# Attention in single-pass high and low parts, one head after another, with the division on GpSimd

## The reference, cut to what matters

```python
q = (_rmsnorm(c_q, q_norm) @ w_uq)          # 8 heads of 64 + 32 (rotary)
kv = (_rmsnorm(c_kv, kv_norm) @ w_ukv)      # 8 heads of 64 (key) + 64 (value)
k_rope = _apply_rope(k_r, cos, sin)         # one for all heads
s = (q_nope . k_nope + q_rope . k_rope) * (64 + 32) ** -0.5
p = softmax(s, axis=-1)                     # rows of 512 keys
o = p @ v
```

## Time and profile before

| | us |
|---|---|
| median of 3 runs | 2398.46 (2389.69 to 2399.76) |
| profiled execution | 2398.28 |
| its span | 2396.6 |
| PE busy (matmul) | 1885.3, 79% |
| DVE (VectorE) | 956.1, 40% |
| ACT (ScalarE) | 609.4, 25% |
| POOL (GpSimd) | 592.5, 25% |

### The profile page before, as it was taken

The page is one execution under the profiler, slowest core; times in us unless marked ns, Lnnn a source line. Parts: engine busy times, 40 slices in busy tenths (PEclk is TensorE's granted clock), DMA queues, the critical chain, the costliest instruction groups (busy, mean ns, idle before and its releaser), DMA issues. The chain is left out here.

```text
span 2396.6 us, 21376 instructions
## 1 busy us (share of the span) xinstructions
PE 1885.3 (79%) x7770; PEld 1285.0 (54%) x7770; DVE 956.1 (40%) x1462; ACT 609.4 (25%) x1006; POOL 592.5 (25%) x292
## 2 busy tenths in 40 slices
PE   4989895839991897997765997199689446999997
PEld 3855432724440683542552443178469335888886
DVE  2814455411115552445540111563366361432332
ACT  2233455001110333445301111212420422111111
POOL 3410024221112430012321110244032022444442
PEclk9989996859995998998767999599779867999998
DMA  4110011148843310010117773231000012222221
GB/s 156 68 63 1 19 53 53 44 190 318 312 158 113 145 44 37 1 44 27 53 45 320 293 304 117 88 126 38 8 1 0 5 70 94 92 96 99 94 88 44
DMA packets 42415, 234.85 MB, mean 98 GB/s; under 512 B 9732, under 2 KB 11652, under 8 KB 22612
## 3 DMA queue, kind: packets, MB, share of 16 engines
q1 hardware_dynamic: 32452, 216.47, 23.9%
q0 software_dynamic: 9728, 16.93, 1.9%
q10 hardware_dynamic: 144, 0.26, 0.1%
HBM read 226.00 MB, written 24.41 MB: 104 GB/s over the span
## 5 line engine op out<-in xcount | busy, mean ns | idle before, releaser
L249 PE MATMUL bank<-XS,WS 128*128 128x512 f32 x864 | 201.4, 396 | 20.0 <-POOL WS L395 20.0
L1958 POOL TENSOR_TENSOR WS<-ring,WS 128x2048 fp32r<-128x2048 f32 x32 | 154.6, 4833 | 228.0 <-ACT WS L1950 228.0
L249 PEld LDWEIGHTS bank<-XS,WS 128*128 128x128 f32 x864 | 165.0, 191 | 56.0 <-POOL WS L395 21.4
L1979 PE MATMUL bank<-XS,WS 128*128 128x512 f32 x768 | 177.2, 393 | 14.5 <-POOL WS L1958 14.5
L1997 PE MATMUL bank<-WS,US 128*128 128x512 f32 x768 | 174.7, 389 | 0.0
L1979 PEld LDWEIGHTS bank<-XS,WS 128*128 128x128 f32 x768 | 145.8, 190 | 45.2 <-issue 14.7
L1997 PEld LDWEIGHTS bank<-WS,US 128*128 128x128 f32 x768 | 144.1, 188 | 29.9
L1384 PE MATMUL bank<-XS,WS 128*128 128x512 f32 (+1 forms) x600 | 138.2, 393 | 14.6 <-POOL WS L1438 14.6
L609 POOL TENSOR_TENSOR RM<-ROW,mask 128x512 f32<-128x512 f32 x32 | 41.5, 1301 | 380.4 <-DMA ROW<-gate_rows 318.9
L1384 PEld LDWEIGHTS bank<-XS,WS 128*128 128x128 f32 (+1 forms) x600 | 112.1, 187 | 40.4 <-POOL WS L1438 14.8
L1950 ACT CAST WS<-ring 128x2048 fp32r<-128x2048 f32 x32 | 61.2, 1913 | 283.5 <-PE bank L1979 150.5
(11 more groups left out here) (438 smaller groups left out, 3179.5 us busy)
## 6 DMA issues: line engine op xcount, KB each, us to landing
raw<-in_w_exp SPq DMA_DIRECT2D x16, 2048.0 KB, 10.2
DN<-in_w_exp SPq DMA_DIRECT2D x32, 1024.0 KB, 4.9
GU<-in_w_exp SPq DMA_DIRECT2D x16, 2048.0 KB, 10.3
ring<-in_w_ff SPq DMA_DIRECT2D x32, 1024.0 KB, 4.8
raw<-in_w_in SPq DMA_DIRECT2D x20, 1024.0 KB, 4.8
ring<-in_w_in SPq DMA_DIRECT2D x12, 1024.0 KB, 4.7
raw<-in_w_out SPq DMA_DIRECT2D x8, 1024.0 KB, 4.9
ROW<-gate_rows SPq DMA_DIRECT2D x32, 256.0 KB, 3.2
```

The lines of the kernel that those rows point to most:

```text
L249: last = pe.matmul(m.ps[g % 8][:, :], WS[:, i % 2, hw, at:at + P], XS[:, hx, k, :], start=(step == 0), stop=(step == 3 * KD - 1))
L1958: pool.tensor_tensor(f.WS[:, q % 2, 1, :], f.ring[:, q % 4, :], f.WS[:, q % 2, 0, :].bitcast(F32), ALU.subtract).then_inc(w_low, 1)
L1979: last = pe.matmul(m.ps[mine + u % 4][:, :], f.WS[:, q % 2, hw, k * 256 + c * P:k * 256 + (c + 1) * P], f.XS[:, hx, k, :], start=(n == 0), ...
```

## The change

- Scores (`scores_of`): queries and keys are held as high and low parts in float32r (`QS`, `KS`), three one-pass matmuls of 512 columns replace one float32 matmul. The key's rotary rows are split once.
- Probabilities with values (`values_of`): `VS` and `PT` are split likewise. Two tiles (256 query columns) are taken together: per pair of tiles 4 blocks of 3 terms, 12 matmuls of 256 columns, done in two parts of 6, one part per step. All the tiles of a head go to one bank `O`, which ScalarE copies home once per head.
- The halves are gone. The heads run one by one: the projection of head h+1 is put among the tiles of head h (query at t = 0, key at t = 1), the values' 4 matmuls among the tiles of head 0.
- New splitting work: ScalarE makes high parts (`query_high` at t = 1, `key_high` at t = 2, `PT` high for each tile), VectorE low parts (`key_low` at t = 2, `PT` low for each tile), GpSimd the query's low part.
- The scale goes into the rotary table once (in `constants`); the maximum is negated by the reduction itself, so that L544 goes.
- The product with the reciprocal (L549) moves from VectorE to GpSimd.
- Three score banks instead of four; three `PT` buffers of two tiles; `w_mla` is put in the upper half of `raw` and is loaded after low part 8 instead of 10, and the quarters of `w_out` go to the lower half.

The core of the new stage, in each engine's order:

```diff
@@ tensor, per step (32 tiles + 6)
+                if step < NI:
+                    scores_of(step)
+                    if t == 0 and h + 1 < HEADS:
+                        query(h + 1)
+                    if t == 1 and h + 1 < HEADS:
+                        key(h + 1)
+                    if h == 0:
+                        value(t)
+                if 2 <= step < NI + 2:
+                    turned(step - 2)
+                if step >= 5:
+                    u, part = divmod(step - 5, 2)
+                    if u < 2 * HEADS:
+                        values_of(u, (2 * part, 2 * part + 1))
@@ values_of
+                if ks[0] == 0:
+                    pe.wait_ge(pt_low, 2 * u + 2)
+                    if u == 0:
+                        pe.wait_ge(v_low, NT)
+                    if half == 0 and h >= 1:
+                        pe.wait_ge(head_home, h)
@@ scalar, start and per step
+            inverse(0, m.ps[1], 128)
+            act.wait_ge(kr_done, 1)
+            act.copy(a.KS[64:128, :, 0, :], ...).then_inc(kr_high, 1)
+            inverse(1, m.ps[0], 256)
+            key_high(0)
+            query_high(0)
...
+                if step >= 10 and step % NT == 2 and step // NT <= HEADS + 1:
+                    hp = (step - 10) // NT
+                    act.wait_ge(pv, 4 * (hp + 1))
+                    act.copy(m.XT[64 * (hp % 2):64 * (hp % 2) + 64, hp // 2, :], O[0:64, :]).then_inc(head_home, 1)
+                if step < NI:
+                    act.wait_ge(neg_max, step + 1)
...
+                    act.activation(PR[:, step % 4, :], m.ps[step % 3][:, :], ACT.Exp, ...).then_inc(probs, 1)
+                    if h == 0:
+                        act.wait_ge(v_done, t + 1)
+                        act.copy(a.VS[:, 0, t, :], O[:, :]).then_inc(v_high, 1)
+                    if h + 1 < HEADS:
+                        if t == 1:
+                            query_high(h + 1)
+                        if t == 2:
+                            key_high(h + 1)
+                if 2 <= step < NI + 2:
+                    act.wait_ge(probs_t, i + 1)
...
+                    act.copy(a.PT[:, u % 3, 0, :, ...], m.ps[4 + i % 2][:, :]...).then_inc(pt_high, 1)
@@ vector, per step
+                    dve.reduce_max(a.NM[...], m.ps[step % 3][:, :], AX.X, negate=True).then_inc(neg_max, 1)
+                    if h == 0:
+                        dve.wait_ge(v_high, t + 1)
+                        dve.tensor_tensor(a.VS[:, 1, t, :], O[:, :], a.VS[:, 0, t, :].bitcast(F32), ALU.subtract).then_inc(v_low, 1)
+                    if h + 1 < HEADS:
+                        if t == 0:
+                            query_home(h + 1)
+                        if t == 2:
+                            key_low(h + 1)
+                if 1 <= step <= NI:
...
+                    dve.reciprocal(a.RC[...], a.SM[...]).then_inc(inv_sum, 1)      # tile step - 1
+                if step >= 2:
...
+                    dve.wait_ge(pt_high, i + 1)                                    # tile i = step - 2
+                    dve.tensor_tensor(a.PT[:, u % 3, 1, ...], m.ps[4 + i % 2]..., a.PT[:, u % 3, 0, ...], ALU.subtract).then_inc(pt_low, 1)
@@ gpsimd
+            query_low(0)
+            for i in range(NI):
+                pool.wait_ge(inv_sum, i + 1)
+                pool.tensor_scalar(PR[:, i % 4, :], PR[:, i % 4, :], a.RC[...], None, ALU.mult).then_inc(probs_normed, 1)
+                if t == 1 and h + 1 < HEADS:
+                    query_low(h + 1)
```

More of the change, by code:

```diff
@@ L441, in _ @@
-            for half in range(2):
-                for hh in range(HH):
-                    h = half * HH + hh
-                    if h == 0:
[L446 to L486, removed]
@@ new lines, in query, with key @@
+            def query(h):
+                if h >= 1:
+                    pe.wait_ge(q_home, h)
+                for k in range(2):
+                    last = pe.matmul(Q[:, :], wq[:, k, h * P:(h + 1) * P], mx.CQ[:, k, :], start=(k == 0), stop=(k == 1))
+                last.then_inc(q_done, 1)
+            def key(h):
+                if h >= 1:
+                    pe.wait_ge(k_low, h)
+                pe.matmul(K[0:64, :], wk[:, h * 64:(h + 1) * 64], mx.CQ[:, 2, :], start=True, stop=True).then_inc(k_done, 1)
@@ new lines, in value, with scores_of @@
+            def value(t):
+                if t >= 1:
+                    pe.wait_ge(v_low, t)
+                pe.matmul(O[:, :], mx.CQ[:, 2, t * P:(t + 1) * P], wv, start=True, stop=True).then_inc(v_done, 1)
+            def scores_of(i):
+                h, t = divmod(i, NT)
+                if t == 0:
+                    pe.wait_ge(k_low, h + 1)
+                    pe.wait_ge(q_low, h + 1)
+                if i == 0:
+                    pe.wait_ge(kr_low, 1)
+                if i >= 3:
+                    pe.wait_ge(probs, i - 2)
+                for n, (hk, hq) in enumerate(TERMS):
+                    last = pe.matmul(m.ps[i % 3][:, :], a.QS[:, h % 2, hq, t * P:(t + 1) * P], a.KS[:, h % 2, hk, :], start=(n == 0), stop=(n == 2))
+                last.then_inc(scores, 1)
@@ new lines, in turned, with values_of @@
+            def turned(i):
+                pe.wait_ge(probs_normed, i + 1)
+                if i >= 2:
+                    pe.wait_ge(pt_low, i - 1)
+                for k in range(NT):
+                    last = pe.transpose(m.ps[4 + i % 2][:, k * P:(k + 1) * P], PR[:, i % 4, k * P:(k + 1) * P], m.ident[:, :])
+                last.then_inc(probs_t, 1)
+            def values_of(u, ks):
+                h, half = divmod(u, 2)
+                if ks[0] == 0:
[4 more added lines that the diff above has]
+                        pe.wait_ge(head_home, h)
+                n = 0
+                for k in ks:
+                    for hv, hp in TERMS:
+                        last = pe.matmul(O[0:64, half * 256:(half + 1) * 256], a.VS[:, hv, k, h * 64:(h + 1) * 64], a.PT[:, u % 3, hp, k, :],
+                                         start=(k == 0 and n == 0), stop=(k == NT - 1 and n == 3 * len(ks) - 1))
+                        n += 1
+                last.then_inc(pv, 1)
@@ L498, in _, with inverse @@
[L498 to L508, removed]
[L509 to L518 removed]
+            def inverse(c, bank, width):
+                act.wait_ge(sums, c + 1)
+                link(act.activation(RS[c], bank[:, :], ACT.Ln, scale=1.0 / width, bias=1e-6))
+                act.activation(RS[c], RS[c], ACT.Exp, scale=-0.5).then_inc(inv_rms, 1)
```

183 lines of the change are left out of this document (107 added, 76 removed).

## The result

The changed kernel takes 2424.11 us (median of 4 runs, 2421.87 to 2425.73) against 2398.72 (4 runs, 2389.69 to 2399.76): ratio 1.0112, 95% interval 1.0092 to 1.0132. It is slower, by more than can be taken for no change, and by less than the 2440 forecast. The profiled execution took 2421.87 us, span 2420.1, which is 23.5 more than the span before.

A forecast was written before the change was run, and what follows sets the result against it. TensorE was taken to bound the attention stage at 2.51 us a tile, with in-order waits binding after the change. 2398.3 + 26.7 (stage) + .5 (table scale) + 15 (clock) = 2440 us; own range 2428 to 2455, 8-in-10 range 2392 to 2468.

The forecast's parts named there:

- the rival in which the clock holds: Rival for the attention stage: TensorE's gaps bring no half clock, so the kernel takes 2425 us; chance .23.
- The two waits: TensorE stalls per head: 1.8 us before values at t = 1 (head copy), 2.5 before transposes at t = 3 (GpSimd's product).
- The product at 1.57: GpSimd's one-operation product of probabilities with the reciprocal, 128x512, was taken to last 1.57 us.
- TensorE's work per tile: Attention tile on TensorE: scores .80, transposes .53, values .87, so 2.20 us instead of 2.51; 11.7 per head with projections.
- my 297.8: Forecast length in us of the attention stage over both layers, 148.9 each, 26.7 over the earlier 271.1.
- The clock: Half clock on TensorE after its gaps, 1.7 us of work lost each; two of three gaps counted, 15 us.
- 16 us from one head's first scores to the next: Sign of being right, in the attention stage's timeline: a head takes 16.0 us against 13.8 before.
- Start and end: Attention stage's edges: 18.0 us to first scores; head 7 10.0 to its last maximum plus a drain of 8.9.
- The other stages: Only the attention stage was to change; any other stage moving by more than 2 us was a sign of being wrong.
- The short terms: Rival: GpSimd's product .77, no change-over between TensorE's groups, 14.4 us per head; 2405, no change; chance .17.
- The half clock feeds itself: Rival: gaps keep TensorE's clock low, 6.8 us more per head over 14 heads, 95 on top; 2520; chance .08.
- TensorE runs ahead: Rival: other engines' chains hide under TensorE's 11.7 us per head and both gaps vanish; 2376, faster; chance .10.

The follow-up runs named there:

- e7: The change plus two useless float32 matmuls on TensorE in its gap before the transposes at t = 3; 2410.05 us, ratio 1.0053.
- e1: The change with ScalarE's copy of a finished head moved from t = 2 to the top of t = 1, ahead of Exp; 2405.19 us.
- e2: The change with VectorE's reciprocal issued ahead of the key's low part at t = 2; 2392.35 us, ratio .9972.
- e3: The change with GpSimd's product written as multiply and add zero, two operations instead of one; 2401.93 us, ratio 1.0007.
- e6: The kernel before the change with only the one-operation product moved to GpSimd; 2416.03 us, ratio 1.0077.
- e10: e9 with VectorE's key low part at t = 2 moved behind the subtraction of the probabilities; 2339.43 us, ratio .9773.
- e5: e4's orders with plain float32 matmuls for scores and values, without high and low parts; 2367.71 us, ratio .9869.
- e9: e4 with VectorE's subtraction for the probabilities' low part one step later; 2363.90 us, ratio .9867.
- e4: The change with the edits of e1, e2 and e3 together; 2362.66 us, ratio .9837.
- e8: e4 with ScalarE's cast of the transposed tile i-2 at the top of the step, ahead of Exp; 2364.18 us, ratio .9858.

## Why the prediction was right, and where it was not

The direction and the mechanism held. The number is 16 us too high (2440 against 2424): for the profiled execution 14 from TensorE's work and 8 from the rest of the program, less 3.5 in terms that I had too low. The time alone would not have shown the mechanism. 2424 lies just outside the forecast's own range (2428 to 2455) and on the number of the rival in which the clock holds (2425); only the windows and e7 part the two.

- **The two waits.** Forecast 1.8 us at t = 1 behind `head_home` and 2.5 at t = 3 behind the reciprocal and the product; measured 1.56 to 1.69 and 2.67 to 2.68, at the instructions named. e1, e2 and e3 each take away one link and 19 to 32 us. The product at 1.57 (1563 ns in the trace) was right too, and e3 and e6 show that it counts.
- **The term that was mis-sized: TensorE's work per tile.** I charged .10 us of change-over on the scores and .14 on the values, left the transposes at .53, and had a tile of 2.20 and a head of 11.7. The trace has .70 + .35 + .78 = 1.83, and 10.40 for a head where nothing waits (e10). Three matmuls of .233 cost just .70, with nothing added, and values follow transposes after .35. In e5 the same transposes with plain float32 values behind them take .53 (188.32 to 188.85), so the .53 of the earlier trace rows belonged to the matmuls that followed. A clean head of the change, at full clock, is 15.1 us (in e7 the values behind the wait at t = 1 start at 208.43, 223.57 and 238.59) where I had 16.0. In e7's layer 1 the seven steps from one head's first maximum to the next take 16.2, 12.8 and five times 15.0 to 15.1, together 104.3, where I had 17.1, 13.3 and five times 16.0, together 110.4. In two layers that is 12 of the 14 us by which the two stages of e7 (141.7 + 141.8 = 283.5) are below my 297.8.
- **The clock.** Forecast 15 us; e7 says 14 by the medians and 17 by the stages. Windows of 1 us from 192 to 286 are below 1.00 in five stretches, behind five of the six waits for the product there (2.67 to 2.89 us); the sixth, 2.68 at 251.75, passed. Layer 2 has five of six as well. Each stretch loses 1.7 us of work, as I had it, but a head with one lasts 16.4 to 16.6 (values behind the wait at t = 1, 212.42 to 229.00 to 245.64, and 260.80 to 277.20) against 15.1, so .2 to .4 of that is hidden. I had counted 9.3 stretches (two of three of 14) at 1.6 to 1.7, and there were 10 at 1.3 to 1.5: that the total is right is partly luck. So is the sign "16 us from one head's first scores to the next": the first maxima of the change are 15.8 to 16.5 apart, but of these 15.0 or 15.1 are the chain and the rest is the half clock, which I had added separately.
- **Start and end.** First scores 16.9 us after the start in layer 1 and 18.3 in layer 2, forecast 18.0. From head 7's first maximum to the stage's end e7's layer 1 takes 19.6, forecast 18.9.
- **The other stages** moved by more than the 2 us that I had named as a sign against me: the rest behind layer 2's stage is 7.9 us shorter. The table shows why this is no effect of the change: e1 and e9 have the long rest with the same code there, and the kernel before has runs of 2389.69 beside 2399.76. It makes the profiled pair look closer by 8 than the edit alone would make it. It goes with the clock behind the stage (.73 or .74 against .76 to .78); what switches that, I can't say, and nothing was tried.
- **The sum.** 2440 less 14.3 for the stage's work, plus 2.3 for the clock, less 7.9 for the rest and with 1.2 more ahead of the stage than I counted, is 2421.3, against 2421.87 measured for that execution. These terms are read off the profiled pair and e7, so the sum has to close; it shows sizes, and proves nothing further.
- **The rivals.** "The clock holds" is out (.92). The short terms were half right: no change-over, but GpSimd at 1.56. "The half clock feeds itself" is out, since the clock came back after 3 to 4 us each time. "TensorE runs ahead", which I took for one chance in ten as the change stands, is what e10 does with three instructions in other places (the key's low part was moved twice) and the product at .69; its 2376 was still too high.

I underrated how much of the loss hung on the order alone. The sum treated each wait as given; the experiments show that the same work, with three instructions moved and the product in its shorter form, is 85 us faster than the change.

## What to carry to other kernels

When work is split over engines, follow each engine's own queue and ask, for every instruction that waits, what short instruction stands behind it and who needs that one: here a reciprocal of .15 us behind a wait of 1.3 cost 32 us, the half clock that followed included. Faster matmuls pay only once TensorE is what binds: the one-pass parts were worth nothing measurable at e4 and 28 us at e10, with the same arithmetic. After each wait removed, look at the timeline again before guessing at the next one; twice (e8, e9) the gap only moved. And check the releaser that a profile names against the program: here the page named VectorE's subtraction in every second head, and the head copy was what the values waited for.

## What was unexpected of the hardware

- GpSimd's product of a 128x512 tile takes 1563 ns with one operation and 692 with two (multiply, then add zero). The earlier trace rows showed such a pair (1566 and 768), but with other operands.
- Useless matmuls in an idle gap made the whole kernel 14 us faster (e7), since the clock stayed at 2.4 GHz.
- The length of a wait alone does not say whether the clock falls behind it. In e2 the clock was at .62, .50, .50 and .68 from 220 to 224, behind the wait of 1.83; in e3 it stayed at 1.00 from 960 to 1030 with five waits of 1.81 before the transposes, and in the change one of 2.68 and one of 2.67 passed. What else counts is open.
